# A hybrid encoder layer: all long products of the recurrence tiles on VectorE, none on GpSimd

## The reference

```
z = rmsnorm(x) @ w_in                          # u_pool, u_lru, u_gate, u_conv
c = depthwise_conv(u_lru, width 4)
for each direction:
    r = sigmoid(c @ wa + ba);  i = sigmoid(c @ wx + bx)     # block diagonal, 8 heads
    a = exp(-8 * r * softplus(-lambda))
    b = sqrt(1 - a*a) * (i * c)
    h[t] = a[t] * h[t-1] + b[t]                # backwards in the other direction
y_lru = (h_fwd + h_bwd) * gelu(u_gate)
x += concat[y_pool, y_lru, y_conv] @ w_out
x += expert_choice_ffn(rmsnorm(x))             # 16 experts
```

## Time and profile before

| what | value |
|---|---|
| median of 3 runs | 2715.28 us (2713.98 to 2718.09) |
| profiled execution, its own time | 2717.59 us |
| its span | 2715.8 us |
| mean granted TensorE clock | 0.961 |
| busy: PE, DVE, ACT, POOL | 2505.3, 1732.7, 1135.2, 491.6 us |

### The profile page before, as it was taken

The page is one execution under the profiler, slowest core; times in us unless marked ns, Lnnn a source line. Parts: engine busy times, 40 slices in busy tenths (PEclk is TensorE's granted clock), DMA queues, the critical chain, the costliest instruction groups (busy, mean ns, idle before and its releaser), DMA issues.

```text
span 2715.8 us, 43040 instructions
## 1 busy us (share of the span) xinstructions
PE 2505.3 (92%) x15942; PEld 2202.1 (81%) x15942; DVE 1732.7 (64%) x2057; ACT 1135.2 (42%) x1552; POOL 491.6 (18%) x347
## 2 busy tenths in 40 slices
PE   6999899989998199999999999999999999999970
PEld 4445455558787199999999999999999999999970
DVE  5499856689355666656755765766666666567534
ACT  5101564543133044444444444444544544454423
POOL 0000033310000112132131231321321321321210
PEclk9999999999998599999999999999999999999995
DMA  5000011126766166776776866866866867767628
GB/s 177 16 16 17 35 53 35 35 97 211 250 225 212 49 176 161 205 197 160 210 186 162 226 168 174 225 165 188 214 164 190 211 159 203 201 159 208 180 65 284
DMA packets 647622, 425.67 MB, mean 157 GB/s; under 512 B 28992, under 2 KB 622144, under 8 KB 646464
## 3 DMA queue, kind: packets, MB, share of 16 engines
q1 hardware_dynamic: 619840, 385.84, 48.6%
q0 software_dynamic: 27648, 37.77, 7.3%
HBM read 357.48 MB, written 66.06 MB: 156 GB/s over the span
## 4 chain that ended last, share of the span: by engine, by line
PE 82%; DVE 11%; issue 2%; DMA 2%; ACT 2%; POOL 0%; SPq 0%; ACTq 0%; DVEq 0%; POOLq 0%
PE ps L1259 41%; PE ps L1276 20%; PE ps L1055 8%; DVE rows L1368 6%; PE ps L1131 4%; PE ps L1146 3%; DMA y<-fin_y 1%; PE ps L1163 1%; PE ps L1009 1%; PE ps L1030 1%; PE ps L1043 1%; DVE over_t L1624 1%; ACT rows L862 1%; DMA mix_in<-mixed 1%; DVE fin_y L1787 0%
## 5 line engine op out<-in xcount | busy, mean ns | idle before, releaser
L1259 PE MATMUL ps<-x_h,w_l 128*128 128x288 f32 x2816 | 830.2, 295 | 20.0 <-issue 20.0
L1259 PE MATMUL ps<-x_l,w_h 128*128 128x288 f32 x2816 | 828.7, 294 | 0.0
L1259 PE MATMUL ps<-x_h,w_h 128*128 128x288 f32 x2816 | 828.6, 294 | 0.0
L1655 DVE TENSOR_TENSOR w_l<-raw,w_h 128x1024 fp32r<-128x1024 f32 (+1 forms) x480 | 637.3, 1328 | 276.7 <-ACT w_h L945 276.1
L945 ACT ACTIVATE w_h<-raw 128x1024 fp32r<-128x1024 f32 (+1 forms) x480 | 545.3, 1143 | 452.9 <-PE ps L1276 272.4
L1259 PEld LDWEIGHTS ps<-x_h,w_l 128*128 128x128 f32 x2816 | 529.0, 188 | 20.0 <-issue 20.0
L1259 PEld LDWEIGHTS ps<-x_l,w_h 128*128 128x128 f32 x2816 | 529.1, 188 | 0.0
L1259 PEld LDWEIGHTS ps<-x_h,w_h 128*128 128x128 f32 x2816 | 529.0, 188 | 0.0
L712 POOL DMA_INDIRECT resid<-y_rows,idx_cur x144 | 250.2, 1737 | 965.0 <-ACT y_rows L960 930.5
L1276 PE MATMUL ps<-h_l,w_h 128*128 128x288 f32 x1408 | 414.0, 294 | 0.0
L1276 PE MATMUL ps<-h_h,w_h 128*128 128x288 f32 x1408 | 414.0, 294 | 0.0
(11 more groups left out here) (221 smaller groups left out, 2436.7 us busy)
## 6 DMA issues: line engine op xcount, KB each, us to landing
raw<-w_gate SPq DMA_DIRECT2D x176, 512.0 KB, 4.3
raw<-w_up SPq DMA_DIRECT2D x176, 512.0 KB, 4.2
raw<-w_down SPq DMA_DIRECT2D x128, 704.0 KB, 5.4
n_x<-x SPq DMA_DIRECT2D x18, 512.0 KB, 4.1
e_x<-x SPq DMA_DIRECT2D x18, 512.0 KB, 5.0
resid<-e_x SPq DMA_DIRECT2D x18, 512.0 KB, 3.2
s_x<-resid SPq DMA_DIRECT2D x18, 512.0 KB, 4.7
resid<-s_r SPq DMA_DIRECT2D x18, 512.0 KB, 3.1
```

Source lines behind the costliest of these rows:

```text
L1259: ins = e.matmul(ps[:, bank, 0:SLOTS], lhs(k), rhs[:, k, 0:SLOTS], start=m == 1, stop=m == 3 * KD)
L1655: e.tensor_tensor(w_l[:, m % SPLIT, 0:k * P], raw[:, m % RAW, 0:k * P], w_h[:, m % SPLIT, 0:k * P].bitcast(F32), ALU.subtract).then_inc(lo ...
```

## The change

GpSimd loses all its products of the recurrence tiles, and the semaphores `ge_arg` and `lru_i` go. VectorE makes them in its own order: the cube right behind the affine, the gated input of a direction right ahead of L1504 of the same direction (it waits for the gate group itself), and the product of u_gate and its Sigmoid ahead of the output product L1521. The arithmetic is the same.

```diff
-            def gelu_cube(l):
-                e.wait_ge(ge_arg, l + 1)
-                e.tensor_tensor(rows[:, 6, mid], rows[:, 6, mid], rows[:, 8, mid], ALU.mult).then_inc(ge_out, 1)
-            def gated(l, d):
-                e.wait_ge(seg_out, NS * (G_LOOP + PER_L * l + 2 * d + 2))
-                it = rows[:, 1 + 3 * d, mid]
-                e.tensor_tensor(it, it, rows[:, 9, mid], ALU.mult).then_inc(lru_i, 1)
-            with e.Fori(0, NLRU - 1) as l:
-                gelu_cube(l)
-                gated(l, 0)
-                gated(l, 1)
-                e.wait_ge(ge_sig, l + 1)
-                e.tensor_tensor(rows[:, 8, mid], rows[:, 8, mid], rows[:, 6, mid], ALU.mult).then_inc(ge_out, 1)
-            gelu_cube(NLRU - 1)
-            gated(NLRU - 1, 0)
...
-                e.wait_ge(ge_out, 2 * l + 1)
+                e.wait_ge(ge_out, l + 1)
                 e.activation(rows[:, 6, LO:HI], rows[:, 6, LO:HI], ACT.Sigmoid).then_inc(ge_sig, 1)
...
-                e.tensor_scalar(rows[:, 6, mid], rows[:, 6, mid], GELU_K * 0.044715, GELU_K, ALU.mult, ALU.add
-                                ).then_inc(ge_arg, 1)
+                step.link(e.tensor_scalar(rows[:, 6, mid], rows[:, 6, mid], GELU_K * 0.044715, GELU_K,
+                                          ALU.mult, ALU.add))
+                e.tensor_tensor(rows[:, 6, mid], rows[:, 6, mid], rows[:, 8, mid], ALU.mult).then_inc(ge_out, 1)
...
                 for d in range(2):
                     r, it = rows[:, 3 * d, mid], rows[:, 3 * d + 1, mid]
+                    e.wait_ge(seg_out, NS * (G_LOOP + PER_L * l + 2 * d + 2))
+                    step.link(e.tensor_tensor(it, it, rows[:, 9, mid], ALU.mult))
                     if last and d == 1:
-                        e.wait_ge(seg_out, NS * (G_LOOP + PER_L * l + 4))
-                        step.link(e.tensor_tensor(it, it, rows[:, 9, mid], ALU.mult))
                         early_sum(4)
-                    else:
-                        e.wait_ge(lru_i, 2 * l + d + 1)
                     e.wait_ge(lru_s, 2 * l + d + 1)
                     step.link(e.tensor_tensor(r, r, it, ALU.mult))
...
-                    e.wait_ge(ge_sig, l + 1)
-                    step.link(e.tensor_tensor(rows[:, 8, mid], rows[:, 8, mid], rows[:, 6, mid], ALU.mult))
-                else:
-                    e.wait_ge(ge_out, 2 * l + 2)
+                e.wait_ge(ge_sig, l + 1)
+                step.link(e.tensor_tensor(rows[:, 8, mid], rows[:, 8, mid], rows[:, 6, mid], ALU.mult))
                 e.tensor_tensor(rows[:, 6, mid], rows[:, 1, mid], rows[:, 8, mid], ALU.mult
                                 ).then_inc(lru_out, 1)
...
                     e.wait_ge(seg_full, NS * (G_LOOP + PER_L * l + 4))
-                    e.wait_ge(lru_i, 2 * l + 2)
                     lru_conv(l + 1)
```

More of the change, by code:

```diff
@@ L336, in encoder_layer @@
         bd_hi, bd_lo, u_hi, u_lo = (sem_of(n) for n in ("bd_hi", "bd_lo", "u_hi", "u_lo"))
-        gate_t, lru_nb, lru_s, lru_i = (sem_of(n) for n in ("gate_t", "lru_nb", "lru_s", "lru_i"))
-        ge_arg, ge_sig, ge_out = (sem_of(n) for n in ("ge_arg", "ge_sig", "ge_out"))
+        gate_t, lru_nb, lru_s = (sem_of(n) for n in ("gate_t", "lru_nb", "lru_s"))
+        ge_sig, ge_out = sem_of("ge_sig"), sem_of("ge_out")
         lru_out = sem_of("lru_out")
@@ L669, in _ @@
             e.memset(rows[:, 0:6, PAD + SAMPLE:PAD + SAMPLE + PAD], 0.0).then_inc(rows_zeroed, 1)
-            mid = slice(LO, HI)
-            def gelu_cube(l):
-                e.wait_ge(ge_arg, l + 1)
-                e.tensor_tensor(rows[:, 6, mid], rows[:, 6, mid], rows[:, 8, mid], ALU.mult).then_inc(ge_out, 1)
-            def gated(l, d):
-                e.wait_ge(seg_out, NS * (G_LOOP + PER_L * l + 2 * d + 2))
-                it = rows[:, 1 + 3 * d, mid]
-                e.tensor_tensor(it, it, rows[:, 9, mid], ALU.mult).then_inc(lru_i, 1)
-            with e.Fori(0, NLRU - 1) as l:
-                gelu_cube(l)
-                gated(l, 0)
-                gated(l, 1)
-                e.wait_ge(ge_sig, l + 1)
-                e.tensor_tensor(rows[:, 8, mid], rows[:, 8, mid], rows[:, 6, mid], ALU.mult).then_inc(ge_out, 1)
-            gelu_cube(NLRU - 1)
-            gated(NLRU - 1, 0)
             def gather(nx):
@@ L1538, in _ @@
             with e.Fori(0, NLRU - 1) as l:
-                step.enter(l, 15)
+                step.enter(l, 19)
                 lru_tile(l, False)
```

## The result

The changed kernel takes 2720.35 us (median of 20 runs, 2718.72 to 2723.6) against 2716.16 us before (median of 20 runs, 2712.25 to 2718.9). The ratio is 1.0017, with a 95% interval of 1.001 to 1.0024: 4.6 us slower by the ratio, 2.7 to 6.5 us by the interval. The forecast was 4.5 us slower. The profiled execution took 2720.18 us, its span 2718.4 us.

A forecast was written before the change was run, and what follows sets the result against it. The prediction took VectorE's order in the last tile as the path. Its terms, 0.4 + 1.3 + 2.6 + 0.2 = +4.5 us, gave a median of 2719.8 us, range 2712.5 to 2723.0.

The forecast's parts named there:

- The bound: Last tile: VectorE's order is the path, continued by SP's queue and transfers; PE's 101 us end 2.9 us too early to matter.
- The loop: Recurrence tiles 1 and 2: `u_lo` 3.5 us later, mostly covered, costing 0.2 us for each tile, +0.4 us together.
- entry rival: Rival: ACT's first evacuation follows PE in the loop too, tiles 1 and 2 cost 1.3 us each; 2722.0 us, chance 0.20.
- The entry: Start of the last tile: late `u_lo` delays PE's first gate segment and ACT's table load, +1.3 us.
- One product more in the stretch: Last tile, VectorE from its first L1489: it also makes the first direction's gated input, +2.6 us.
- The clock: Later output projection: first matmuls slower after PE's gap grows from 2.9 to 5.1 us at most, +0.2 us.
- The tail: SP's stores and loads after the last tile: 4.3 us of delay carried over in full to the later output projection.
- The head: Start of the early output projection: PE starts near 607 instead of 609.6, a 2.6 us gain not on the path.
- PE binds: Rival: PE bounds the early projection, so its 2.6 us gain stays and only 0.4 is lost; 2713.1 us, chance 0.08.
- the stall was on the path: Rival: L1453's 5 us stall and up to 1.9 us of slow matmuls come off the chain; 2708.8 us, chance 0.05.
- the transfers absorb: Rival: transfers after the last tile find emptier engines and catch up about 3 of 4.3 us; 2716.8 us, chance 0.10.
- VectorE becomes the bound: Rival: all 14 products on the path, less the stalls relieved, +18.5 us; 2733.8 us, chance 0.05.

The follow-up runs named there:

- last_only: Kernel before with GpSimd's products moved to VectorE only in the last tile, GpSimd keeping those of tiles 0 to 2; 2719.35 us, ratio 1.0008 to before.
- four_more: Changed kernel with four further long products, not affecting the output, in VectorE's stretch of the last tile; 2732.39 us, ratio 1.0056 to before.
- gated0_early: Changed kernel with the last tile's first gated input made right behind the cube, no longer in VectorE's stretch; 2716.48 us, ratio 1.0005 to before.
- gelu_off_pool: Kernel before with only the gelu product of tiles 0 to 2 moved from GpSimd to VectorE's idle time; 2714.59 us in a single run.
- all_early: Changed kernel with all gated inputs and gelu products made ahead of each tile's first L1489, last tile included; 2711.97 us, ratio 0.9985 to before.
- loop_only: Kernel before with GpSimd's products moved to VectorE only in tiles 0 to 2, the last tile as before; 2719.86 us, ratio 1.0011 to before.

## Why the prediction was right

**The bound.** That the last tile's VectorE order is the path although the chain view gives 101 us to PE, and that SP's queue carries a delay on: shown by last_only (PE's early projection 78.3 us after the last projection stretch began, against 82.0 before, and no gain), by four_more (10.45 us in, 10.6 us more by the ratios, 15.2 against 4.6) and by gated0_early (the 2.6 us out of the stretch again). PE isn't far behind: in gelu_off_pool its early run ends 1.02 us before the later projection starts.

**The loop.** Predicted +0.2 us for each of tiles 1 and 2, with ends of nothing and 1.4. Measured 0.38 each (76.75 against 76.37), 0.8 in all: the cover was there, the size was half. PE starts the gates of tile 1 at 437.87, right behind `u_lo` (437.61) and after a gap of 1.59 us that was not there before. ACT's load for the Sigmoid starts 64.30 us after the projection stretch before it began (438.47 - 374.17), exactly as in the kernel before (439.09 - 374.79), so the late gates don't delay it. The loss comes behind it. PE's gate matmuls now run without a gap, where before they waited 1.08 us for ACT:

```profile
437.87 12.83 PE L1023 MATMUL ps<-u_parts,bd_parts 128*128 128x512 f32 x60 [1.59 <-DVE u_parts L1378]
```

ACT's 15 evacuations take 8.53 us and not 8.14. In the third group they come every 0.69 us and no longer every 0.57, and PE's three matmuls of a segment take 0.65 to 0.7: there ACT has caught up with PE. The prediction had 0.4 us from PE's lateness as the most and halved it.

Its border for the entry rival, `u_lo` later than 438.3, was drawn too early. It asked that the first segment be there when ACT's load starts. In the changed kernel the third matmul of the segment ends at 438.83, 0.36 us after the load started, and nothing is lost by that: in the loop the load doesn't wait for the segment, and ACT needs it only at 439.76. In the last tile ACT has one load and not two, and it starts behind the wait for the segment (592.23), so the delay is paid there: 1.65 us.

**The entry.** Predicted +1.3 us, measured +1.65 (64.53 against 62.88). The hand-over from `u_lo` (591.12) to PE (591.21) is 0.09 us and the table load follows at 592.23: PE's first segment and the hand-over to ACT took 1.0 us after the gap, where I had 0.70 from matmuls in full flow. all_early brings `u_lo` ahead of PE's need and the term is gone: shown.

**One product more in the stretch.** Predicted 2.6 us, measured 2.60 (57.84 against 55.24).

**The clock.** I added 0.2 us for slow matmuls after a longer gap. The gap grew from 2.92 to 3.30 us only, and the first 24 matmuls took 7.32 us against 7.38: nothing.

**The tail.** The delay was to be carried over in full, and four_more shows that it is. Two signs missed all the same: `out_half` was to start at about 718.3 behind a PE gap of 4 to 5 us, and it started at 716.57 behind 3.30. The forecast put the 4.3 us on top of the tail of one profile, 42.97 us from the store, and no other profile with transfers at the end has one that long (40.7 to 41.9).

**The sum** by stretches is 0.8 + 1.65 + 2.6 = 5.0 us against the forecast's 4.5. The profiles have 4.4 us at the store of sum 8, because the changed kernel's tile 0 began 0.6 us earlier, and the runs have 4.6 (2.7 to 6.5). That the median came within 0.6 us of the forecast 2719.8 is partly luck: the two costs that were too small and the clock that was too large partly cancel, the median that it started from, of three runs, was 0.9 us below that of twenty, and the interval of the difference is 3.8 us wide.

**The head.** PE was to start near 607: 607.64. It stayed worthless, as argued. `u_lo` net +3.5 us: `u_lo` of the last tile ended 59.83 us after the start of the projection stretch before (587.38 - 527.55) and 63.42 us in the changed kernel (591.12 - 527.70), 3.6 us more. Two readings were off without weight: the low halves gave back 6.0 us and not 5, since the first of them had stood too, and the chain came to them 7.7 us after the table load and not 6 (598.17 - 590.43).

**The rivals.** "The entry is paid in every tile" is out by the tile distance; "PE binds" and "the stall was on the path" by last_only; "the transfers absorb" by four_more; "VectorE becomes the bound", as priced with all 14 products on the path, by the tile distance and the 4.6 us. In a weaker sense it came true: the chain of tiles 1 and 2 goes round through VectorE's stretch, at a price of 0.38 us a tile. VectorE's 14.7 us of idle time in a tile don't speak against that, since it waits there for ACT, and ACT in part for the gates that `u_lo` released. What one more product in the loop would cost is not shown. PE does become the bound of the last stage in all_early, with 5 us less in VectorE's stretch.

What stays open: the times of loop_only and last_only, 3.0 and 2.2 us above before by their ratios, are each uncertain by 2.5 us, so the separate prices of the terms rest on the stretches in the profiles, not on times. Why the tail took 42.97 us in the profile of the kernel before, and 40.7 to 41.9 us in the others where transfers set it, was not settled.

## What to carry to other kernels

When work moves to a faster engine, price the place in that engine's order, not the engine: the same 14 products cost 4.6 us behind the waits of the recurrence and nothing in the idle time ahead of it. The 4.1 us gained there came from two products that VectorE had made all along. Where a chain view gives a long gapless stretch to one engine, look at what ended the wait behind it before taking that engine for the bound. A cover that hides a late hand-over in the turns of a loop (here ACT's table loads) need not be there at the loop's exit.

## What the runs showed of the hardware

VectorE and GpSimd, both on float32 operations with two inputs, hand over at instruction ends, and both ways. A VectorE operation issued during GpSimd's stood until that one ended (6.87 us for 2.57), and GpSimd's product issued 0.9 us before VectorE was done took 5.91 us for 5.1 (gelu_off_pool). A low half of w_out of 1.21 us took up to 6.18 us the same way. So a profile counts a blocked engine as busy: about 18.6 us of VectorE's 1732.7 were such standstill. Getting them back made `u_lo` 4.3 us earlier in the loop tiles (gelu_off_pool). At the low halves it let PE start its early projection 3.7 us earlier in last_only, and no time came of it.
